# Last pair normalised early, other load orders, and softplus and scan moved into the input projection

## The chip, the cores and the metric

One NeuronCore of a Trainium2 chip runs the whole program. TensorE (PE) multiplies, VectorE (DVE) and ScalarE (ACT) do elementwise work, GpSimd (POOL) and SyncE (SP) mostly issue DMAs. The metric is the device time of one execution in microseconds (us), lower is better.

## What is computed

One inference step of a one-layer hybrid decoder, over 64 sample rows and a prompt of 1024 rows with 16 learned tokens ahead (1152 columns `T` in the kernel, padding among them):

```python
u = rmsnorm(h, norm_mix)
p = u @ w_in                       # conv, shift, gate and dt columns
dt = softplus(dt_raw + dt_bias);  A = -exp(a_log)
acum = cumsum(dt * A)              # within chunks of 128
y_a = rmsnorm((ssd(xs, dt, acum, B, C) + d_skip * xs) * silu(z), ssm_norm)
y_b = (groupnorm(rwkv7(r, decay, k, v, kk, a)) * lnx_w + lnx_b + bonus) * g
h = h + concat(y_a, y_b) @ w_out
h = h + peer(rmsnorm(h))           # product-key experts
y = rmsnorm(h)
```

Outputs are y and the new convolution, shift, SSD and WKV states.

## The kernel before

The program is a row of stages; between two of them all engines meet at a barrier, and SBUF is handed on. Activations lie transposed: 128 channels on the partitions, time in the columns. float32 products are made of three matmuls on rounded halves (`product`, lines 106 to 109: hi*hi, lo*hi, hi*lo); ScalarE makes the rounded high part, DVE the low part.

**Input projection** (`input_projection`, lines 116 to 397). 27 weight tiles of 128 output columns: 8 conv, 14 shift, 4 gate, 1 dt. For each, TensorE makes 72 matmuls of 384 columns (three column blocks `c`, eight row tiles `k`, three each) into one of two PSUM buffers. `over_tiles` hands every engine the same tile order, mostly in loops. SP first loads the norm weights, the eight x tiles and coefficients, then one weight tile at a time. For x tile `k` ScalarE rounds (L243) and squares (L247), DVE makes the low part (L277) and adds pairs of squares (L285), and TensorE sums them over the partitions (L367) into the PSUM buffer of tile 1. In tile 0 the products of block `c=0` follow the x tiles as they come; blocks 1 and 2 come after the last sum. DVE then builds the inverse root mean square (L288, L291), and in `column_work` makes the low part of the next tile's weights (L302) before it scales the finished tile. POOL stores each finished tile to the scratch tensor `cols`.

**SSD** (`ssd_heads`). DVE and ScalarE first form softplus(dt), its decay and a running sum (`tensor_tensor_scan`, L662) on 8 partitions. TensorE waits for that (`dt_step`), spreads the running sums over rows (L790), and turns `dt` and `cum` to rows by 2 x 9 small matmuls (L799, 18 instructions each). Nine chunks of 128 follow.

**RWKV** (`rwkv_heads`). Four head pairs `j`, each with five groups of one or two chunks; a group's triangular inverse takes six merges `l`, and `at_point(l - 0.5)` and `at_point(l)` put other work between them in a fixed order written out per engine. For a pair `j < 3` the group normalisation (mean, centering, square, variance, root, reciprocal, scaling, gating) is placed among the merges of the next pair. The last pair has none behind it, so `tail` does it all at the end: DVE runs `center`, `variance`, `inverse`, `scaled`, `gated` over three column thirds (`thirds`, 384 columns). Semaphores `ep_pe`, `ep_act` and `ep_vec` count these steps, and `reached` turns a step's name to a count.

**Output projection** (`output_projection`, lines 1827 to 1950). SP loads the eight mixed tiles `u` (`y_d`) and then the residual input (`h`, `h_rest`); POOL loads the weight tiles. ScalarE rounds weights 0 and 1, then the eight y tiles. DVE splits weight 0 and the y tiles, waits for `x_loaded` (the residual), and in `add` splits the next weights before it adds a tile to the residual. TensorE does column chunk by column chunk.

The rest (picking experts, spreading gates, experts with 2 x 3 x 2048 matmuls of 352 columns) isn't touched.

Of the kernel before, what the change touches and what calls it, by code (L numbers as in the profile page):

```python
# [26 lines left out]
P = 128  # L27
# [11 lines left out]
IN_TILES = CONV_TILES + SHIFT_TILES + GATE_TILES + 1  # L39
COEFS_IN = 8  # L40
# [75 lines left out]
def input_projection(nc, x_t, norm_g_d, w_pack, coef_d, hist_d, cols_d, new_conv_s, new_conv_p, new_shift_s, new_shift_p):  # L116
    with Stage(nc, "inp") as st:
# [11 lines left out]
        raw = [sb(f"raw_{s}", [P, E_COLS]) for s in range(2)]  # L129
        mid = [sb(f"mid_{s}", [P, T]) for s in range(2)]  # L130
# [19 lines left out]
        edge_stored = [sem(f"edge_stored_{s}") for s in range(2)]  # L150

# [25 lines left out]
        with nc.Block() as block:  # L177
            @block.sync
            def _(sp):
                sp.dma_start(norm_g[:], norm_g_d).then_inc(g_loaded, 16)  # L180
                for k in range(KD):
# [12 lines left out]
            def _(pool):  # L194
# [13 lines left out]
                def store(q, s, m, kind):  # L208
# [17 lines left out]
                    elif kind == "dt":  # L226
                        pool.wait_ge(gate_ready, START + GATE_TILES + 1)
                    else:
                        pool.wait_ge(act_out, START + (m + 1 if kind == "conv" else m + 1 - SHIFT_TILES))
# [9 lines left out]
            def _(act):  # L239
                act.wait_ge(g_loaded, START + 16)  # L240
                for k in range(KD):
                    act.wait_ge(x_loaded[k], START + 16)
                    act.activation(u_hi[:, k, :], u[:, k, :], ACT.Copy, scale=norm_g[:, k:k + 1]).then_inc(u_rounded, 1)  # L243
# [3 lines left out]
                    act.activation(squares[:, k % 4, :], u[:, k, :], ACT.Square).then_inc(square_ready, 1)  # L247
                    if k == 0:
                        act.wait_ge(w_loaded[0], START + 16)
                        act.activation(w_hi[0][:], w[0][:], ACT.Copy).then_inc(w_rounded, 1)  # L250
                act.wait_ge(rms_step, START + 3)
                act.activation(inv_rms[:], inv_rms[:], ACT.Sqrt).then_inc(rms_step, 1)

                def evacuate(q, s, m, kind):
                    if kind != "dt":
# [17 lines left out]
            def _(dve):  # L273
                dve.wait_ge(g_loaded, START + 16)
                for k in range(KD):
# [6 lines left out]
                    if k % 2:  # L282
                        dve.wait_ge(square_ready, START + k + 1)
                        pair = squares[:, k % 4, :]
                        dve.tensor_tensor(pair, squares[:, k % 4 - 1, :], pair, ALU.add).then_inc(pair_ready, 1)  # L285
# [13 lines left out]
                def column_work(q, s, m, kind):  # L299
                    if kind != "dt":  # L300
                        dve.wait_ge(w_rounded, START + m + 2)
                        dve.tensor_tensor(w_lo[1 - s][:], w[1 - s][:], w_hi[1 - s][:], ALU.subtract).then_inc(w_split, 1)  # L302
                    first = isinstance(m, int) and m < 2
                    if kind not in ("conv", "shift"):
# [57 lines left out]
            def _(pe):  # L362
# [7 lines left out]
                def project(q, s, m, kind):  # L370
# [7 lines left out]
                    else:  # L378
# [3 lines left out]
                        else:  # L382
                            pe.wait_ge(raw_ready, START + CONV_TILES + SHIFT_TILES)
                            pe.wait_ge(gate_ready, START + m - (CONV_TILES + SHIFT_TILES) - 1)
                    for c in range(3):
                        for k in range(KD):
                            if first and c == 0:
                                pe.wait_ge(u_split, START + k + 1)
# [2642 lines left out]
```

## Time and profile before

| | us |
|---|---|
| timed runs, median of 3 | 4183.31 (4179.56 to 4183.43) |
| profiled execution, its time | 4152.66 |
| profiled execution, its span | 4151.1 |
| TensorE busy | 3681.1 (89%) |
| DVE busy | 3275.7 (79%) |
| ScalarE busy | 1166.0 (28%) |

The mean granted TensorE clock is 0.936 of full. In the profile a line such as `49.73 0.59 PE L107 ... [3.10 <-DVE ...]` reads: start 49.73 us, duration 0.59 us, engine and source line, then the engine's idle time before it and what ended that. The stages lie at about 0 to 378 us (input projection), 383 to about 545 (SSD), up to 1287 (RWKV), 1292 to 1430 (output projection), then picking, spreading and, from about 2110, experts.

### The profile page before, as it was taken

To read this page: it belongs to the slowest core of one execution; us is meant where nothing else is said; L and a number is where in the kernel's file an instruction comes from. 1 tells how busy PE (TensorE), PEld (TensorE's weight loads), DVE (VectorE), ACT (ScalarE), POOL (GpSimd) and SP (SyncE) were. 2 spreads that over 40 slices of the span, in tenths; PEclk is the share of its full clock that TensorE was granted. 3 is DMA by queue.
4 is the path that set the end of the run, shared out by engine and by line. 5 is a ranking of instruction groups with operands and counts; after the bars stand their busy time and mean duration, and the time that the engine had idled before them with its cause. 6 is when DMAs were issued, how large, how long until landed. Compare 5 with 4: busy or idle time off the path is not lost. (4 is left out here: it accounts for less than half of the span.)

```text
span 4151.1 us, 65513 instructions
## 1 busy us (share of the span) xinstructions
PE 3681.1 (89%) x22408; PEld 3397.2 (82%) x22408; DVE 3275.7 (79%) x6449; ACT 1166.0 (28%) x2129; POOL 1228.1 (30%) x1086
## 2 busy tenths in 40 slices
PE   7997849889895897847769999999999999999997
PEld 6997727777784755537769999999999999999996
DVE  6542746676663389989969999999999999999998
ACT  3102423223221121229932222222222222222221
POOL 1220000000000000000025555555555555555553
PEclk9998758988997999869989999999999999999998
DMA  4573220000003000104478888888888888888885
GB/s 111 89 93 95 76 89 6 23 28 12 1 9 122 22 25 32 52 1 177 196 287 300 297 286 301 294 285 301 290 289 298 295 290 300 292 292 300 288 296 186
DMA packets 291701, 729.32 MB, mean 176 GB/s; under 512 B 27416, under 2 KB 138472, under 8 KB 290048
## 3 DMA queue, kind: packets, MB, share of 16 engines
q0 software_dynamic: 120448, 431.42, 32.4%
q1 hardware_dynamic: 171136, 296.44, 21.1%
q8 instruction: 61, 1.00, 0.1%
q14 instruction: 56, 0.46, 0.0%
HBM read 650.07 MB, written 77.70 MB: 175 GB/s over the span
## 5 line engine op out<-in xcount | busy, mean ns | idle before, releaser
L2565 POOL DMA_INDIRECT experts_u_row<-in_up_rows,experts_u_at x384 | 540.0, 1406 | 642.7 <-DVE experts_dot L2751 527.8
L107 PE MATMUL experts_up_ps<-experts_u_hi,experts_up_hi 128*128 128x352 f32 x2048 | 662.1, 323 | 27.5 <-DVE experts_u_lo L2727 24.8
L107 PE MATMUL experts_down_ps<-experts_act_hi,experts_down_hi 128*128 128x352 f32 x2048 | 676.5, 330 | 8.6 <-DVE experts_down_lo L2727 6.4
L108 PE MATMUL experts_up_ps<-experts_u_lo,experts_up_hi 128*128 128x352 f32 x2048 | 660.9, 323 | 0.0
L109 PE MATMUL experts_up_ps<-experts_u_hi,experts_up_lo 128*128 128x352 f32 x2048 | 660.6, 323 | 0.0
L108 PE MATMUL experts_down_ps<-experts_act_lo,experts_down_hi 128*128 128x352 f32 x2048 | 660.5, 323 | 0.0
L109 PE MATMUL experts_down_ps<-experts_act_hi,experts_down_lo 128*128 128x352 f32 x2048 | 659.8, 322 | 0.0
L2572 POOL DMA_INDIRECT experts_v_row<-in_down,experts_v_at x384 | 513.9, 1338 | 244.8 <-issue 117.6
L2751 DVE CUSTOM_DVE_ANT_0 experts_u_row<-experts_u_row,stream_u_rows_of 128x1024 f32<-128x1024 f32 x384 | 466.3, 1215 | 73.8 <-DMA experts_u_row<-in_up_rows,experts_u_at 72.3
L2764 DVE SCALAR_TENSOR_TENSOR stream_h_rows_of<-experts_v_row,experts_weight,stream_h_rows_of 128x1024 f32<-128x1024 f32 x384 | 497.6, 1296 | 14.4 <-DVE experts_weight L2756 6.8
L2770 DVE TENSOR_TENSOR stream_h<-stream_h,experts_down_ps 128x704 f32<-128x704 f32 x512 | 450.4, 880 | 65.7 <-PE experts_down_ps L109 65.0
L107 PEld LDWEIGHTS experts_down_ps<-experts_act_hi,experts_down_hi 128*128 128x128 f32 x2048 | 385.3, 188 | 35.7 <-DVE stream_h L2770 25.6
L107 PEld LDWEIGHTS experts_up_ps<-experts_u_hi,experts_up_hi 128*128 128x128 f32 x2048 | 385.9, 188 | 30.1 <-issue 22.1
L108 PEld LDWEIGHTS experts_up_ps<-experts_u_lo,experts_up_hi 128*128 128x128 f32 x2048 | 386.4, 189 | 0.0
L109 PEld LDWEIGHTS experts_up_ps<-experts_u_hi,experts_up_lo 128*128 128x128 f32 x2048 | 386.3, 189 | 0.0
L108 PEld LDWEIGHTS experts_down_ps<-experts_act_lo,experts_down_hi 128*128 128x128 f32 x2048 | 386.0, 188 | 0.0
L109 PEld LDWEIGHTS experts_down_ps<-experts_act_hi,experts_down_lo 128*128 128x128 f32 x2048 | 385.7, 188 | 0.0
L2669 ACT ACTIVATE experts_down_hi<-experts_down 128x1024 fp32r<-128x1024 f32 x128 | 135.1, 1055 | 707.9 <-PE experts_down_ps L109 707.9
L2682 ACT ACTIVATE experts_act_v<-experts_up_ps 128x352 f32<-128x352 f32 x256 | 118.8, 465 | 594.2 <-PE experts_up_ps L109 450.3
L2064 PE MATMUL pick_q_ps<-picking_u,pick_w_query 128*128 128x384 f32 (+1 forms) x768 | 252.6, 490 | 25.9 <-DMA pick_sub_keys<-in_keys 17.4
L2064 PEld LDWEIGHTS pick_q_ps<-picking_u,pick_w_query 128*128 128x128 f32 x768 | 150.9, 199 | 118.2 <-issue 41.3
L107 PE MATMUL inp_proj<-inp_u_hi,inp_w_in_hi 128*128 128x384 f32 x648 | 219.5, 339 | 24.9 <-DVE inp_w_in_lo L281 20.2
(396 smaller groups left out, 6497.7 us busy)
## 6 DMA issues: line engine op xcount, KB each, us to landing
experts_up<-in_up SPq DMA_DIRECT2D x128, 512.0 KB
experts_down<-in_down SPq DMA_DIRECT2D x128, 512.0 KB
gates<-spread_spread SPq DMA_DIRECT2D x11, 4096.0 KB, 11.5
experts_gates<-gates SPq DMA_DIRECT2D x64, 704.0 KB
cols<-inp_done POOLq DMA_DIRECT2D x27, 576.0 KB
inp_w_in<-in_w_in SPq DMA_DIRECT2D x27, 512.0 KB
pick_w_query<-in_w_query SPq DMA_DIRECT2D x16, 512.0 KB
experts_u_row<-in_up_rows,experts_u_at POOLq DMA_INDIRECT x384
```

The costliest lines, as they stand in the source:

```text
L107: pe.matmul(out, w_hi, x_hi, start=start, stop=False)
L108: pe.matmul(out, w_hi, x_lo, start=False, stop=False)
L109: return pe.matmul(out, w_lo, x_hi, start=False, stop=stop)
L2064: mm = pe.matmul(q_ps[at_q % 3][:, 0:n], w[s][:, k * P:k * P + P], u[:, k, lo:lo + n], start=(k == 0), stop=(k == KD - 1))
L2565: pool.indirect_dma_start(u_row[b][:], None, up_rows_d, bass.IndirectOffsetOnAxis(ap=u_at[slot][:, b, a:a + 1], axis=0)).then_inc(u_row_lo ...
L2572: pool.indirect_dma_start(v_row[b][:], None, v_table, bass.IndirectOffsetOnAxis(ap=v_at[slot][:, b, a:a + 1], axis=0)).then_inc(v_row_load ...
L2669: act.activation(down_hi[:, e, :], down[e][:], ACT.Copy).then_inc(down_rounded, 1)
L2682: act.activation(act_v[e][:, lo:lo + n], up_ps[e][c][:, 0:n], ACT.Gelu).then_inc(gelu_ready, 1)
L2751: dve.tensor_tensor_reduce(u_row[b][:], u_row[b][:], rows.u[:, b, :], 1.0, 0.0, ALU.mult, ALU.add, dot[slot][:, b, a:a + 1]).then_inc(dott ...
L2764: dve.scalar_tensor_tensor(out=rows.h[:, b, :], in0=v_row[b][:], scalar=weight[slot][:, b, a:a + 1], in1=rows.h[:, b, :], op0=ALU.mult, op ...
L2770: dve.tensor_tensor(row, row, down_ps[m % 2][:, :, 0:DC], ALU.add).then_inc(added, 1)
```

## The change

Four things are changed.

1. *Input projection*: the first weight tile is loaded right after the first x tile; ScalarE squares one x tile behind the rounding; tile 0 is multiplied x tile by x tile for all three column blocks, and the sums of squares lie between those.
2. *dt tile*: it is made before the gate tiles instead of after them; the gate tiles are written out instead of looped. Softplus, decay and scan of dt are done in this stage, on 8 partitions of the x buffer, among the gate tiles. dt and running sum are stored together as 16 rows, and the SSD stage loads them as one tile `dt_cum`; its turning matmuls take both at once (9 instead of 18), and `head_row` has 16 rows.
3. *RWKV, last pair*: mean and variance of the first two thirds go in among the last group's merges; the tail roots, inverts, scales and gates these 768 columns while the last two chunks are computed, and stores them early. The last third follows.
4. *Output projection*: SP loads weight tile 0, then the y tiles, then weight tile 1, then the residual, and also the later weights (POOL did). ScalarE rounds the y tiles before weight tile 1, and tile 0 is multiplied y tile by y tile for all column chunks.

The diff, cut to its core (renamed indices, packing of the weights and the like left out):

```diff
-            for kind, tiles in (("conv", CONV_TILES - 2), ("shift", SHIFT_TILES), ("gate", GATE_TILES)):
+            for kind, tiles in (("conv", CONV_TILES - 2), ("shift", SHIFT_TILES)):
                 with eng.Fori(lo, lo + tiles // 2) as q:
                     for s in range(2):
                         body(q, s, q * 2 + s, kind)
                 lo += tiles // 2
-            body(lo, 0, 2 * lo, "dt")
+            body(lo, 0, DT_TILE, "dt")
+            for m in range(GATE0, IN_TILES):
...
-                for k in range(KD):
+                sp.dma_start(u[:, 0, :], x_t[0]).then_inc(x_loaded[0], 16)
+                sp.dma_start(w[0][:], w_pack[0]).then_inc(w_loaded[0], 16)
+                for k in range(1, KD):
...
+                    if isinstance(m, int) and m == 1:
+                        sp.dma_start(dt_par[:], dt_par_d).then_inc(par_loaded, 16)
+
+                        sp.wait_ge(u_split, START + KD)
+                        sp.wait_ge(sum_done, START + KD // 2)
+                        sp.dma_start(keep, keep_d[0:HEADS, :]).then_inc(par_loaded, 16)
...
+                        pool.wait_ge(dt_step, START + 6)
+                        pool.dma_start(cols_d[m, 0:2 * HEADS, :].rearrange("(a h) t -> h a t", a=2), u[0:HEADS, 0:2, :]).then_inc(stored[s], 16)
+                        return
...
+                    else:
+                        square(k - 1)
+                square(KD - 1)
...
+                    if kind == "dt":
+                        act.wait_ge(par_loaded, START + 32)
+                        act.activation(dt_par[:, 1:2], dt_par[:, 1:2], ACT.Exp).then_inc(dt_act, 1)
+                        act.wait_ge(dt_step, START + 1)
+                        act.activation(dt_abs, dt, ACT.Abs).then_inc(dt_act, 1)
+                        act.wait_ge(dt_act, START + 2)
+                        act.activation(dt_abs, dt_abs, ACT.Exp, scale=-1.0).then_inc(dt_act, 1)
...
+                        if m == GATE0:
+                            act.wait_ge(dt_step, START + 2)
+                            act.activation(dt_abs, dt_abs, ACT.Ln).then_inc(dt_act, 1)
...
+                    if kind == "gate" and m == GATE0:
+                        dve.wait_ge(dt_act, START + 3)
+                        dve.tensor_scalar(dt_abs, dt_abs, 1.0, None, ALU.add).then_inc(dt_step, 1)
+                    if kind == "gate" and m == GATE0 + 1:
+                        dve.wait_ge(dt_act, START + 4)
+                        dve.scalar_tensor_tensor(out=dt, in0=dt, scalar=0.0, in1=dt_abs, op0=ALU.max, op1=ALU.add).then_inc(dt_step, 1)
+                        dve.wait_ge(dt_step, START + 3)
+                        dve.memset(dt[:, NS:P - META], 0.0).then_inc(dt_step, 1)
+                        dve.wait_ge(dt_step, START + 4)
+                        dve.tensor_scalar(log_decay, dt, dt_par[:, 1:2], -1.0, ALU.mult, ALU.mult).then_inc(dt_step, 1)
+                        dve.wait_ge(dt_step, START + 5)
+                        dve.tensor_tensor_scan(cum, keep, log_decay, 0.0, ALU.mult, ALU.add).then_inc(dt_step, 1)
...
+                    if first:
+
+                        for k in range(KD):
+                            pe.wait_ge(u_split, START + k + 1)
+                            for c in range(3):
+                                one(c, k)
+                            if k % 2 == 0 and k:
+                                sum_of_squares(k - 1)
+                        sum_of_squares(KD - 1)
+                        return
...
-                pe.wait_ge(dt_step, 6)
+                pe.wait_ge(dt_loaded, 16)
...
-                        for a, src in enumerate((dt, cum)):
-                            for t in range(NT):
-                                mm = pe.matmul(small_ps[:, a, t, :], src[:, tile_cols(t)], eye[0:HEADS, 0:HEADS], start=True, stop=True)
+                        for t in range(NT):
+                            mm = pe.matmul(by_row_ps[:, t, :, :].rearrange("p a h -> p (a h)"), dt_cum[:, tile_cols(t)], eye[0:2 * HEADS, 0:2 * HEADS],
+                                           start=True, stop=True)
...
+EARLY_PE = {"mean0": 0.5, "var0": 2.5, "mean1": 3.5, "var1": 5}
+EARLY_ACT = {"square0": 1.5, "square1": 4.5}
+EARLY_VEC = {"mean0": 1, "var0": 3, "mean1": 4, "var1": 5.5}
+LAST_MADE = {
+    EP_PE: (*EARLY_PE, "mean2", "var2"),
+    EP_ACT: (*EARLY_ACT, "rooted_early", "square2", "rooted"),
+    EP_VEC: (*EARLY_VEC, "inverse0", "inverse1", "scaled_early", "affine_early", "with_bonus_early", "gated_early",
+             "mean2", "var2", "inverse2", "scaled", "affine", "with_bonus", "gated"),
+}
...
+                    if j == PAIRS - 1:
+                        first_col = 2 * CH
+                        pool.wait_ge(ep_vec, reached(EP_VEC, j, "gated_early"))
+                        pool.dma_start(y_out[:, 0:NS], y_of[x][:, 0:NS]).then_inc(y_stored, 16)
+                        pool.dma_start(y_out[:, NS:NS + first_col - P], y_of[x][:, P:first_col]).then_inc(y_stored, 16)
...
+                    root(last.j, "var1", slice(0, 2 * CH))
                     for a in range(2):
                         copy_rhs(last.ci + a)
                         copy_u(last.ci + a)
                         copy_y(last, a)
-                    for c in range(3):
-                        square(last.j, c)
-                    root(last.j)
+                    square(last.j, 2)
+                    root(last.j, "var2", slice(2 * CH, T))
...
+                    j, early, rest = last.j, slice(0, 2 * CH), slice(2 * CH, T)
+                    inverse(j, 0)
+                    next_state(last, 0)
+                    inverse(j, 1)
+                    scaled(j, early, "inverse1")
+                    next_state(last, 1)
+                    affine(j, early, "_early")
+                    gated(j, early, "_early")
                     center(j, 2)
                     variance(j, 2)
-                    for c in range(3):
-                        inverse(j, c)
-                    scaled(j)
-                    gated(j)
+                    inverse(j, 2)
+                    scaled(j, rest)
+                    affine(j, rest)
...
+                sp.dma_start(w[0][:], w_out_d[0]).then_inc(w_loaded[0], 16)
                 for k in range(KD):
                     sp.dma_start(u[:, k, :], y_d[k]).then_inc(y_loaded[k], 16)
+                sp.dma_start(w[1][:], w_out_d[1]).then_inc(w_loaded[1], 16)
                 sp.dma_start(h[:], x_kept_d[:, :, 0:DENSE].rearrange("k p t -> p k t")).then_inc(x_loaded, 16)
                 sp.dma_start(h_rest[:], x_kept_d[:, :, DENSE:KEPT].rearrange("k p t -> p k t")).then_inc(x_loaded, 16)
+
+                def load(q, s, m):
+                    if isinstance(m, int) and m < 2:
+                        return
+                    sp.wait_ge(w_split, START + m - 1)
+                    sp.dma_start(w[s][:], at(w_out_d, m)).then_inc(w_loaded[s], 16)
+
+                over_tiles(sp, load)
 
...
-                            mm = product(pe, out[s][c][:, 0:n], w_hi[s][:, cut], w_lo[s][:, cut],
-                                         y_hi[:, k, lo:lo + n], y_lo[:, k, lo:lo + n], k == 0, k == KD - 1)
-                        mm.then_inc(out_done, 1)
+                            pe.wait_ge(y_split, START + k + 1)
+                            for c in range(len(OUT_CHUNKS)):
+                                one(c, k)
+                        return
+                    for c in range(len(OUT_CHUNKS)):
+                        for k in range(KD):
+                            one(c, k)
...
-                    if isinstance(m, int) and m == 1:
+                    if isinstance(m, int) and m == 0:
                         for k in range(KD):
                             act.wait_ge(y_loaded[k], START + 16)
                             act.activation(y_hi[:, k, :], u[:, k, :], ACT.Copy).then_inc(y_rounded, 1)
```

## Rows read from the trace of the kernel before

**Rows 1.** The page of the profile, section 1, its busy times

```profile
PE 3681.1 (89%) x22408; PEld 3397.2 (82%) x22408; DVE 3275.7 (79%) x6449; ACT 1166.0 (28%) x2129; POOL 1228.1 (30%) x1086
```

**Rows 2.** Busy time, granted clock and DMA of four stretches, with the header

```profile
core 0: us, PE busy (x) PEld busy (x) DVE busy (x) ACT busy (x) POOL busy (x), PEclk, DMA share, GB/s
10.00:12.00 2.00, 0.00 (x0) 0.00 (x0) 0.00 (x0) 0.00 (x0) 0.00 (x0) 1.00 1.01 408
110.00:170.00 60.00, 60.00 (x348) 60.00 (x348) 37.22 (x58) 8.47 (x8) 14.48 (x21) 1.00 0.52 95
400.00:420.00 20.00, 18.30 (x87) 17.35 (x86) 7.99 (x18) 9.24 (x23) 0.00 (x0) 0.50 0.02 5
1240.00:1245.00 5.00, 5.00 (x47) 4.71 (x47) 2.18 (x6) 1.78 (x6) 0.00 (x0) 1.00 0.01 3
```

**Rows 3.** Timeline of ACT and DVE, 0 to 50 us (start, duration, engine, line)

```profile
5.66 1.28 ACT L243 ACT_TABLE_LOAD   x1 [5.66 <-DMA inp_u<-in_x_t]
17.85 1.06 ACT L250 ACTIVATE inp_w_in_hi<-inp_w_in 128x1024 fp32r<-128x1024 f32 x1 [8.59 <-DMA inp_w_in<-in_w_in]
...
34.40 1.28 ACT L252 ACT_TABLE_LOAD   x1
38.34 1.49 DVE L288 TENSOR_SCALAR inp_inv_rms<-inp_proj 128x384 f32<-128x384 f32 x3 [2.30 <-PE inp_proj L367]
41.06 7.35 DVE L291 RECIPROCAL inp_inv_rms<-inp_inv_rms 128x1152 f32<-128x1152 f32 x1 [1.24 <-ACT inp_inv_rms L252]
48.45 1.23 DVE L302 TENSOR_TENSOR inp_w_in_lo<-inp_w_in,inp_w_in_hi 128x1024 fp32r<-128x1024 f32 x1
```

**Rows 4.** Timeline of PE, 26 to 56 us

```profile
27.47 2.10 PE L367 MATMUL inp_proj<-inp_squares,inp_in_ones 128*128 128x384 f32 x6
...
49.73 0.59 PE L107 MATMUL inp_proj<-inp_u_hi,inp_w_in_hi 128*128 128x384 f32 x1 [3.10 <-DVE inp_w_in_lo L302]
...
53.31 0.34 PE L109 MATMUL inp_proj<-inp_u_hi,inp_w_in_lo 128*128 128x384 f32 x1
```

**Rows 5.** Timeline of ACT at 95 us and of POOL at 378 us

```profile
95.35 1.17 ACT L265 ACTIVATE inp_done<-inp_mid 128x1152 f32<-128x1152 f32 x1 [10.35 <-DVE inp_mid L343]
...
378.07 0.53 POOL L230 DMA_DIRECT2D cols<-inp_done  x1 [10.38 <-DVE inp_done L297]
```

**Rows 6.** Start of the SSD stage: timeline of PE and SP, then DMA issues

```profile
396.96 3.78 PE L790 MATMUL ssd_rows_ps<-ssd_cum,ssd_head_row 8*128 8x128 f32 x16 [19.78 <-DVE ssd_cum L662]
400.53 3.84 PE L799 MATMUL ssd_shared_ps<-ssd_eye,ssd_dt 8*128 8x8 f32 x18
387.40 0.43 SPq L556 DMA_DIRECT2D ssd_ssd_par<-in_ssd_par  x1
ssd_xbc<-cols SPq DMA_DIRECT2D x3, 512.0 KB, 4.8
```

**Rows 7.** End of the RWKV stage: timeline of ACT, DVE and POOL

```profile
1253.33 0.28 ACT L1202 ACTIVATE rwkv_rhs<-rwkv_chain_ps 128x128 f32<-128x128 f32 x1 [1.42 <-PE rwkv_chain_ps L1662]
...
1264.66 0.29 DVE L1438 TENSOR_TENSOR rwkv_s<-rwkv_s_new_part,rwkv_s_kept 128x128 f32<-128x128 f32 x1
1272.68 7.38 DVE L1463 RECIPROCAL rwkv_inv_decay<-rwkv_inv_decay 128x384 f32<-128x384 f32 x3 [1.23 <-ACT rwkv_inv_decay L1228]
...
1281.48 0.88 DVE L1470 TENSOR_SCALAR rwkv_y<-rwkv_y,rwkv_pair_par 128x1152 f32<-128x1152 f32 x1
...
1283.79 1.36 DVE L1477 TENSOR_TENSOR rwkv_y<-rwkv_y,rwkv_gate 128x1152 f32<-128x1152 f32 x1
1286.03 0.54 POOL L1127 DMA_DIRECT2D mixed<-rwkv_y  x1
```

**Rows 8.** Output projection: timeline of SP and DVE

```profile
1292.41 3.86 SPq L1858 DMA_DIRECT2D picking_u<-mixed  x8
...
1321.51 1.23 DVE L1924 TENSOR_TENSOR outp_w_out_lo<-outp_w_out,outp_w_out_hi 128x1024 fp32r<-128x1024 f32 x1 [5.12 <-DMA picking_h_rest<-in_x_kept]
...
1325.20 0.55 DVE L1945 TENSOR_TENSOR picking_h_rest<-picking_h_rest,outp_out 128x384 f32<-128x384 f32 x1 [1.60 <-PE outp_out L109]
```

More of the change, by code:

```diff
@@ L129, in input_projection @@
         raw = [sb(f"raw_{s}", [P, E_COLS]) for s in range(2)]
+        dt_par = sb("dt_par", [HEADS, 2])
+        dt, cum, keep, dt_abs, log_decay = (u[0:HEADS, k, :] for k in range(5))
         mid = [sb(f"mid_{s}", [P, T]) for s in range(2)]
@@ L254, in evacuate @@
                 def evacuate(q, s, m, kind):
-                    if kind != "dt":
+                    if not (isinstance(m, int) and m == IN_TILES - 1):
                         act.wait_ge(w_loaded[1 - s], START + (q + 1 + s) * 16)
@@ L274, in _, with add_pair @@
                 dve.wait_ge(g_loaded, START + 16)
+                def add_pair(k):
+                    dve.wait_ge(square_ready, START + k + 1)
+                    pair = squares[:, k % 4, :]
+                    dve.tensor_tensor(pair, squares[:, k % 4 - 1, :], pair, ALU.add).then_inc(pair_ready, 1)
                 for k in range(KD):
@@ L299, in column_work @@
                 def column_work(q, s, m, kind):
-                    if kind != "dt":
+                    if not (isinstance(m, int) and m == IN_TILES - 1):
                         dve.wait_ge(w_rounded, START + m + 2)
@@ L789, in rows @@
                     for hh in range(HEADS):
-                        mm = pe.matmul(rows_ps[:, hh, :], head_row[:, hh, :], cum[:, tile_cols(c)], start=True, stop=True)
+                        mm = pe.matmul(rows_ps[:, hh, :], head_row[:, hh, :], dt_cum[:, tile_cols(c)], start=True, stop=True)
                     mm.then_inc(rows_done, 1)
@@ L1262, in at_point @@
                         root(group.j - 1)
+                    if after is None:
+                        for c in range(2):
+                            if point == EARLY_ACT[f"square{c}"]:
+                                square(group.j, c)
                 def tail(last):
+                    root(last.j, "var1", slice(0, 2 * CH))
                     for a in range(2):
@@ L1508, in at_point @@
                             scaled(group.j - 1)
+                            affine(group.j - 1)
                         if point == 5:
                             gated(group.j - 1)
-                def tail(last):
-                    for a in range(2):
-                        next_state(last, a)
-                    j = last.j
-                    center(j, 0)
-                    center(j, 1)
-                    variance(j, 0)
-                    variance(j, 1)
+                    if after is None:
+                        for c in range(2):
+                            if point == EARLY_VEC[f"mean{c}"]:
+                                center(group.j, c)
+                            if point == EARLY_VEC[f"var{c}"]:
+                                variance(group.j, c)
+                def tail(last):
+                    j, early, rest = last.j, slice(0, 2 * CH), slice(2 * CH, T)
[6 more added lines that the diff above has]
+                    gated(j, early, "_early")
                     center(j, 2)
                     variance(j, 2)
-                    for c in range(3):
-                        inverse(j, c)
-                    scaled(j)
-                    gated(j)
+                    inverse(j, 2)
+                    scaled(j, rest)
+                    affine(j, rest)
+                    gated(j, rest)
                 over_groups(dve, prepare, start, merge, at_point, tail)
@@ L1768, in at_point @@
                             start_from_samples(after)
+                    else:
+                        for c in range(2):
+                            if point == EARLY_PE[f"mean{c}"]:
+                                mean(group.j, c)
+                            if point == EARLY_PE[f"var{c}"]:
+                                variance(group.j, c)
                     if group.g == 0 and group.j > 0:
@@ L1781, in tail @@
                         make_state(last, a)
-                    j = last.j
-                    mean(j, 0)
-                    mean(j, 1)
-                    variance(j, 0)
-                    variance(j, 1)
-                    mean(j, 2)
-                    variance(j, 2)
+                    mean(last.j, 2)
+                    variance(last.j, 2)
                 over_groups(pe, prepare, start, merge, at_point, tail)
```

183 lines of the change are left out of this document (86 added, 97 removed).

## The prediction

> **What bounds the kernel now.** Read the page first [rows 1]: TensorE is busy 89% of the span, so only what shortens TensorE's path, or the gaps in it, moves the end. The table of stretches [rows 2] says where it is the bound: 110 to 170 us (steady input projection) holds 348 matmuls back to back, 0.172 us each, 12.4 us for the 72 of a weight tile, at the full level (1.00, 2.4 GHz). There an edit on another engine is worth nothing. The change works at four places where TensorE waits for a chain on other engines: the input projection's head [rows 3, 4], the seam to the SSD stage [rows 5, 6], the RWKV stage's end [rows 7], the output projection's head [rows 8]. Experts, picking and the middle of every stage are left as they are, so gains at seams go straight into the time.
>
> **Input projection, head.** Now the first weights land behind all eight x tiles, and ScalarE rounds them at 17.85; the last sum of squares is read at 38.34; 3 column passes (1.49), root, reciprocal (7.35) and the low part of tile 1's weights (1.23) follow, and TensorE starts tile 1 at 49.73 after 3.10 idle [rows 3, 4]. After: x0 lands at 5.66 as now; at 408 GB/s [rows 2] 512 KB take 1.3 us and 576 KB 1.45 us, so w0 is there at 7.0 and the last x at 17. ScalarE: x0 (begun 6.9) 1.2, w0 1.06, DVE's low part 1.23 (behind the 1.4 us x0 pass): TensorE starts at 11. All 72 products of tile 0 (12.4 us) and 24 matmuls of sums (2.10 for six [rows 4], 8.4) now lie before the last sum: 20.8 us. The start is at the half level (1.2 GHz); [rows 4] show one such start: matmuls of 0.59 at 49.73 and of 0.34 at 53.31, thus some 3.6 us at half speed, 1.8 us lost. Sum read at 11 + 20.8 + 1.8 = 33.6. ScalarE isn't later: its remaining passes took 34.40 - 18.9 = 15.5 us, and from 9.2 would end near 26. Gain 38.34 - 33.6, taken as 4.8 (the 2.10 holds some pipeline tail). The chain behind it stays serial, so tile 1 moves by the same 4.8. Its gap grows from 3 to 11.5 us, but 3.1 us already cost the fall to the half level, so I add nothing. Ends: 3 (half level for 7 us) and 6.5.
>
> **The dt tile and softplus, moved.** Tile 22 is now dt, gates are 23 to 26. SP issues one keep load (after the last sum) and dt_par; tile 2's weight load waits behind them to about 36 and is needed only when tile 2's weights are rounded, near 53. ScalarE gets Exp, Abs, Exp, Ln with table loads (1.28 each [rows 3]) and DVE about 6 us: in tiles of 12.4 us, where DVE is busy 37 of 60 us in the conv tiles [rows 2] and less in gate tiles; next tile's weight split comes before this work on DVE, and the first rounding behind it on ScalarE is ready some 6 us into the tile. POOL's dt store waits for the scan, and gate tile 23's store queues behind it; DVE's tile 24 waits for that landing, about 10 of 12.4 us into the tile. Cost nothing; without that cover a few us. But the last tile is now a gate: its Silu (1.17) and hand-off lie between the last product and the last store, which went at 378.07 straight from DVE [rows 5]. Cost 1.2.
>
> **SSD head.** TensorE starts at 396.96, released by the scan, after 19.78 idle [rows 6]. After, it waits for dt_cum and six constants. The last of them was issued at 387.40, with two loads fewer ahead now 386.8; the strided 512 KB load just ahead of it takes 4.8 to land [rows 6] from 385.8, or 390.6. I take 390.8: gain 6.2. Ends: 2 us after issue (+7.6 rather than 6.2), 7 us after (+3). Then 18 matmuls of 8x8 in 3.84 us [rows 6] vanish: the two rows of 18 become one. Gain 3.8; TensorE is at half level there (0.50 [rows 2]) and the next ScalarE copy waits for it, so it is on the path. The level stays low after: the gap is still 14 us.
>
> **RWKV, end.** Now the last state is ready at 1264.95, then mean, square, variance, root, three reciprocals (7.38) and four full-width passes in a row, ending 1283.79 + 1.36 = 1285.15 [rows 7]. After, statistics of two thirds lie in the last group's six merges. There TensorE is full (5.00 of 5 us, 0.95 of it weight loads [rows 2]), so the eight added matmuls cost: at 0.35 each [rows 4] 2.8, less the pauses they fill and pipelining; I take 2.2, ends 0.8 and 4. ScalarE does the early root (two thirds of 1.17 is 0.8, behind a 0.6 variance) before the copy that ran at 1253.33 [rows 7], and the whole chain of the last two chunks queues behind that: 1.1. State ready at 1264.95 + 3.3 = 1268.3. Two reciprocals (2.46 each) and the scaling fit in DVE's waits for TensorE. Then DVE runs the early affine and gating ahead of the last centering (0.6 + 1.8), then per third: center 0.56, square 0.52, variance matmuls 1.0, read 0.56, root 0.52, reciprocal 2.46, four passes 1.8, and 0.6 of hand-offs: 10.4, end 1278.7. Gain 6.4. The store is one POOL issue (0.54) shorter and smaller, about 0.5: 7.5 in all. Ends 4 and 10.
>
> **Output projection, head.** The tempting sum is large: weights first and row by row, tile 0 would end some 10 us sooner. But the second tile's low part is released at 1321.51 by the landing of the residual input (DVE idle 5.12 <- DMA picking_h_rest [rows 8]), since DVE's queue holds that wait ahead of the split. Its landing is set by bytes: y, two weight tiles and 4.25 MB of residual. Only the third weight tile (512 KB, 1.3 us) now comes behind it. So tile 1 starts near 1321.4 instead of the end of tile 0 (1325.0, read by the row at 1325.20): 3.5. Tile 0 ends about 1314.5, TensorE idles 7 us and restarts at the half level, 1.7 by [rows 4]. Gain 1.8. Ends 0.5 and 4. The Trainium skill, "TensorE: Matmul & The Clock Gate", section "HAM oscillation — how this bites in real kernels", warns of the order used here: matmul bursts parted by waits for transfers can run cold each time. By that rule tile 0, whose rows come one transfer at a time, would run at the half level throughout and end near 1324 instead of 1314.5, with no gap behind it: a gain of 1 to 2, much as above. The trace shows one cold restart after one gap and no repeated ones.
>
> **Sum.** 4.8 - 1.2 + 6.2 + 3.8 + 7.5 + 1.8 = 22.9 us. The profiled execution (span 4151.1, time 4152.66) would go to 4129.8. The timed runs have a median of 4183.31, 30.6 us above it, which the profile doesn't explain; I carry the difference over: 4183.3 - 22.9 = **4160.4**.
>
> **Rivals.**
> (a) *The overlaps are thinner*: the last constant lands 7 us after issue (-3.2), the merges take the full 4 us (-1.8) and the output head gives 0.5 (-1.3), the input head 3 (-1.8): gain 14.8, time 4168.5; with the early root holding up the chain by 3 us more, 4171.5. For it: TensorE is full in 1240 to 1245 [rows 2]. Against: all four at once.
> (b) *The output projection keeps its full gain*, because the residual isn't what ends last there: 9 us instead of 1.8, time 4153. For it: TensorE would be ready. Against: the release in [rows 8].
> (c) *Slower by the clock*: the two new long gaps (11.5 and 7 us) are followed by stretches that stay at the half level. From 400 to 420 us TensorE was busy 18.3 of 20 us and still at 0.50 [rows 2]. A dense tile at that level costs 12.4 us more; two tiles behind each gap make 49.6 less the 3.5 counted: 4206. It turns the sign from 46 us at half speed more than counted (23 lost). Against: the dense restart of [rows 4] was back at 53.31.
> (d) *It hardly shows*: the 30.6 us between the profiled and the timed runs move with something outside the edits and swallow it: 4180.
>
> **How the numbers follow.** Forecast 60% (4154 to 4166), (a) 18%, (b) 8%, (d) 10%, (c) 4%. A measurement tells 0.2%, 8.4 us, from no change. Faster: 60 + 18 + 8 = 86%, and 1 of (d): 87%. Same 9%, slower 4%. The range leaves out (c) and most of (d), and takes in (a)'s end and a little beyond (b): 4147 to 4175.
>
> **What the profile after would show.** Sum read near 33.6, tile 1 at 45, with half-level matmuls behind both; DVE's scan inside the gate tiles and no TensorE gap there; SSD's first matmul within some 8 us of that stage's first load, then 18 small matmuls, not 36; the last gating pass about 10 us behind the last state, where it now ends 20 us behind it, and one POOL issue after it; DVE still released by picking_h_rest before tile 1, with TensorE idle 7 us. It would be wrong if a matmul gap opened inside the tiles 22 to 26, if the last constant or the residual landed elsewhere than taken, or if TensorE stayed low after a gap.

## The result

| kernel, job | median (us) | runs from .. to | ratio to before, 95% |
|---|---|---|---|
| before, first job | 4183.37 | 4179.56 .. 4186.96 | |
| after, first job | 4149.69 | 4144.40 .. 4155.00 | 0.992 (0.9905 to 0.9935) |
| before, second job | 4155.67 | 4147.42 .. 4160.22 | |
| after, second job | 4126.44 | 4125.25 .. 4134.40 | 0.9939 (0.9925 to 0.9953) |

The forecast was 4160.4, a gain of 22.9 us, with a range of 4147 to 4175. The first job gives 33.7 us (27 to 40 by the interval), the second 25.3 (20 to 31). The forecast time was 11 us too high; the gain agrees with the second job.

**The profile after** (its own time 4148.04, span 4146.5). First the input projection's head, timeline of PE and DVE (start, duration, engine, line, tiles, idle time before and what ended it):

```profile
31.68 2.10 PE L431 MATMUL inp_proj<-inp_squares,inp_in_ones 128*128 128x384 f32 x6
...
45.20 0.69 PE L109 MATMUL inp_proj<-inp_u_hi,inp_w_in_hi 128*128 128x384 f32 x1 [11.42 <-DVE inp_w_in_lo L344]
33.82 1.49 DVE L330 TENSOR_SCALAR inp_inv_rms<-inp_proj 128x384 f32<-128x384 f32 x3 [4.94 <-PE inp_proj L431]
36.53 7.35 DVE L333 RECIPROCAL inp_inv_rms<-inp_inv_rms 128x1152 f32<-128x1152 f32 x1 [1.23 <-ACT inp_inv_rms L279]
43.92 1.23 DVE L344 TENSOR_TENSOR inp_w_in_lo<-inp_w_in,inp_w_in_hi 128x1024 fp32r<-128x1024 f32 x1
```

The sum is read at 33.82 and tile 1 starts at 45.20; forecast were 33.6 and 45, against 38.34 and 49.73 in [rows 3, 4]. The seam to SSD, PE and SP:

```profile
411.79 3.75 PE L834 MATMUL ssd_rows_ps<-ssd_dt_cum,ssd_head_row 16*128 16x128 f32 x16 [14.60 <-DMA ssd_ssd_par<-in_ssd_par]
415.34 3.86 PE L842 MATMUL ssd_shared_ps<-ssd_eye,ssd_dt_cum 16*128 16x16 f32 x18
419.12 1.11 PE L849 MATMUL ssd_x_ps<-ssd_eye,ssd_xbc 128*128 128x128 f32 x4
404.81 0.33 SPq L605 DMA_DIRECT2D ssd_dt_cum<-cols  x1
```

TensorE is now released by a constant, not by the scan of [rows 6], 6.98 us after the stage's first load, and one row of 18 small matmuls is left. The RWKV end, DVE and POOL, which answers [rows 7]:

```profile
1273.75 0.29 DVE L1503 TENSOR_TENSOR rwkv_s<-rwkv_s_new_part,rwkv_s_kept 128x128 f32<-128x128 f32 x1
...
1280.53 2.55 DVE L1528 RECIPROCAL rwkv_inv_decay<-rwkv_inv_decay 128x384 f32<-128x384 f32 x1 [0.59 <-ACT rwkv_inv_decay L1289]
...
1284.82 0.56 DVE L1545 TENSOR_TENSOR rwkv_y<-rwkv_y,rwkv_gate 128x384 f32<-128x384 f32 x1
1285.67 0.58 POOL L1188 DMA_DIRECT2D mixed<-rwkv_y  x1 [6.61 <-DVE rwkv_y L1545]
```

From the last state (1273.75) to the last gating pass (start 1284.82) it is 11.07 us, where [rows 7] have 19.13, and one issue follows. The output projection's head, SP, PE and DVE, which answers [rows 8]:

```profile
1291.54 0.33 SPq L1936 DMA_DIRECT2D outp_w_out<-in_w_out  x1
1299.69 0.63 PE L109 MATMUL outp_out<-outp_y_hi,outp_w_out_hi 128*128 128x352 f32 x1 [20.35 <-DVE outp_y_lo L2021]
1320.84 0.66 PE L109 MATMUL outp_out<-outp_y_hi,outp_w_out_hi 128*128 128x352 f32 x1 [7.67 <-DVE outp_w_out_lo L2016]
1319.56 1.23 DVE L2016 TENSOR_TENSOR outp_w_out_lo<-outp_w_out,outp_w_out_hi 128x1024 fp32r<-128x1024 f32 x1 [10.38 <-DMA picking_h_rest<-in_x_kept]
```

As forecast, tile 1 waits 7.67 us for the residual input's landing through VectorE's queue. All that stands as the prediction has it. One thing doesn't. Busy time and granted clock by stretch, after:

```profile
core 0: us, PE busy (x) PEld busy (x) DVE busy (x) ACT busy (x) POOL busy (x), PEclk, DMA share, GB/s
150.00:200.00 50.00, 50.00 (x290) 50.00 (x289) 22.31 (x36) 4.25 (x4) 8.84 (x13) 1.00 0.83 82
200.00:250.00 50.00, 46.75 (x267) 45.81 (x266) 19.34 (x33) 3.17 (x3) 11.37 (x16) 1.00 0.81 83
250.00:300.00 50.00, 44.30 (x243) 43.26 (x242) 19.68 (x31) 4.23 (x4) 9.43 (x14) 0.97 0.75 85
300.00:350.00 50.00, 39.29 (x216) 39.00 (x216) 19.18 (x31) 4.84 (x6) 10.47 (x15) 0.90 0.81 77
```

From 200 us on TensorE is no longer full in the shift tiles, which the change leaves alone. Six gaps between 210 and 296 us make 8.95 us, and one of 10.71 stands at the start of tile 22, the dt tile. PE and DVE there:

```profile
332.72 0.66 PE L109 MATMUL inp_proj<-inp_u_hi,inp_w_in_hi 128*128 128x384 f32 x1 [10.71 <-issue]
331.07 0.23 DVE L389 TENSOR_TENSOR inp_raw<-inp_proj,inp_inv_rms 128x64 f32<-128x64 f32 x1 [9.12 <-DMA inp_raw<-in_hist]
```

The SSD stage's first load is at 404.81, where before has 383.49. The input projection thus lost 21 us in this profile although its head gained, and yet the timed runs gained 34. This had to be explained first.

### The profile page after: what moved, and what is told of

The parts are those of the page before. It is cut to its first block and busy times, and to the rows that moved or that the text cites. A ratio compares the mean times of both kernels' runs of the same rounds, so it can differ in the third digit from the quotient of the medians.

```text
span 4146.5 us, 65409 instructions
## 1 busy us (share of the span) xinstructions
PE 3671.6 (89%) x22390; PEld 3391.5 (82%) x22390; DVE 3275.0 (79%) x6453; ACT 1167.4 (28%) x2131; POOL 1226.1 (30%) x1079
## 6 DMA issues: line engine op xcount, KB each, us to landing
gates<-spread_spread SPq DMA_DIRECT2D x11, 4096.0 KB, 11.5
```

## Experiments

**Whose are the gaps, and which part gains what.** e1 is before unchanged, e2 after unchanged, e3 and e4 the two halves of the change. All four ran on one chip.

> The kernel before, once more, for its trace on the chip of the other runs. Theory A (the gaps of TensorE in the shift tiles, some 24 us between 200 and 345 us in the profile after, belong to the chip: its small transfers are slower): they stand in this trace as well, the last product of the input projection ends 20 to 40 us later than in the profile before (377), and the time is near 4180. Theory B (the changed order of loads or the tile moved makes them): no gaps here, the input projection ends near 377 and the time is near 4153.

> The kernel after, once more. Theory A: the gaps in the shift tiles are as in e1, and the ratio to before is 0.994 (23 us, the sum of the prediction). Theory B: the gaps are here alone, the gain is what is left of 23 us after them, a few us.

> Only the changes of the input projection (order of loads, row by row, softplus and scan there) and of the SSD head; the RWKV end and the output projection as before. By the sum of the prediction 4.8 - 1.2 + 6.2 + 3.8 = 13.6 us faster than before. If the moved work slows the tiles (Theory B) it is 5 us faster or slower than before.

> Only the RWKV end and the output projection; the rest as before. By the sum 7.5 + 1.8 = 9.3 us faster. If the two traces read so far are right that the output projection's stage is as long as before, 7.5; if the merges pay their full four us and the projection nothing, 5.

```diff
 # e3: rwkv_heads and output_projection as before, the rest as after
 # e4: rwkv_heads and output_projection as after, the rest as before
```

Measured: e1 4161.08 (one run). e2 0.9939. e3 4138.97, 0.9961 (0.9948 to 0.9975), 16.2 us faster, for 13.6 expected. e4 4148.44, 0.9984 (0.9975 to 0.9993), 6.7 us faster, for 9.3 expected by the sum, or 7.5 or 5; its interval, 3 to 10 us, doesn't choose among them. The halves add up to 22.9, e2 has 25.3. The same stretches in e2:

```profile
150.00:200.00 50.00, 50.00 (x290) 50.00 (x289) 22.93 (x37) 4.25 (x4) 11.04 (x16) 1.00 0.63 91
200.00:250.00 50.00, 50.00 (x291) 50.00 (x290) 22.85 (x37) 4.25 (x4) 11.40 (x16) 1.00 0.71 91
250.00:300.00 50.00, 50.00 (x290) 50.00 (x289) 22.75 (x37) 4.25 (x4) 11.36 (x16) 1.00 0.72 92
300.00:350.00 50.00, 49.30 (x285) 49.01 (x284) 20.73 (x28) 12.10 (x12) 6.83 (x10) 1.00 0.42 70
```

The same code has no gaps here, so the moved tile and the new order of loads don't make them (theory B falls). e1 has none before 300 us either, and its time is 4161 and not 4180, so theory A doesn't hold for this chip. It is the first job that was slower, for both kernels (before by 28 us, after by 23). What differs is a chain in GpSimd's queue. In each conv and shift tile it waits for the previous tile's columns to land, loads the next tile's history (12 byte pieces), stores two edges and then the columns; VectorE can't scale the next tile before that history is there, and its split of the weights after that stands behind the scaling in its queue: it is such a split (L344) that ends the six smaller gaps. Of the 22 history loads that follow the first one, the second and the last, in after and in e2:

```profile
61.59 0.91 POOL L222 DMA_DIRECT2D inp_raw<-in_hist  x1 [7.46 <-DMA cols<-inp_done]
340.85 0.91 POOL L222 DMA_DIRECT2D inp_raw<-in_hist  x1 [9.99 <-DMA cols<-inp_done]
```

```profile
61.20 0.95 POOL L222 DMA_DIRECT2D inp_raw<-in_hist  x1 [7.28 <-DVE inp_raw L339]
313.70 0.91 POOL L222 DMA_DIRECT2D inp_raw<-in_hist  x1 [8.17 <-DMA cols<-inp_done]
```

Over 20 tiles that is 13.96 us a tile in after and 12.62 in e2; in before it is 12.74 and in e1 12.62. A tile's products take 12.48 us. So in each of these profiles the chain is slower than TensorE, and eats up the lead that it starts with. At 12.62 that costs e2 nothing yet: the gap in its last row is 0.70 us at the dt tile, and e9 to e11 below have the same 0.70 there without the chain's wait. At 13.96 the lead is gone by 210, and the stage ends 24.3 us later (404.81 against 380.53).

Why the largest gap stands at the dt tile is in the code. In the shift tiles TensorE waits for the scaling of the tile before the last one (`raw_ready`, `m - 1`), at the dt tile for that of the last shift tile (`CONV_TILES + SHIFT_TILES`), so whatever VectorE lags behind shows there in full: in the two lines above it scales until 332.6, and TensorE starts at 332.72. The kernel before has the same wait at its first gate tile. The dt tile writes the PSUM buffer that tile 20 used, so the looser wait looks sufficient there; no run tried it.

**Does that chain do it?** e7 and e8 lengthen it by one more small load a tile, in after and in before.

```diff
                         pool.dma_start(at(out_p, i), raw[s][:, E_COLS - HIST:E_COLS]).then_inc(edge_stored[s], 16)
+                        load_spare(s, m)      # hist_d[m] once more, into a spare buffer
```

> The kernel after, with one more small transfer (a second load of the 12 byte pieces of the history, into a spare buffer) in each of the 22 conv and shift tiles, so that the chain of small transfers in GpSimd's queue is longer. Theory A (the gaps of the shift tiles in the first profile of after come from this chain, once it is longer than a tile's 12.48 us): gaps of the same kind appear here, of 1 to 3 us a tile in the 14 shift tiles, 15 to 40 us in all. Rival: the chain has more slack, the tiles stay back to back and the time is after's.

> The kernel before with the same extra transfer. Theory A (the chain is no part of the change): it loses as much as e7 does against after, within 5 us. Theory B (the change brought the kernel nearer to this edge): before loses at least 10 us less than after does.

Measured: e7 4134.47, 0.9959 (0.9944 to 0.9974), against 0.9939 without the load: 8 us lost. e8 4158.41, 1.0014 (1.0004 to 1.0024): 6 us lost. In both the period is 13.03 and the SSD stage's first load comes later, at 387.06 for e7 (e2 380.53) and 389.29 for e8 (e1 384.53). Gaps inside the shift tiles, as theory A of e7 has them, don't come: the chain grew by 0.4 us a tile only, and TensorE waits once, at the start of tile 22, for 4.34 us in e7 (0.70 in e2) and 5.29 in e8 (0.84 in before), behind a history load. The loss is smaller than the 15 us expected as the least. It is alike in both kernels within the intervals, so nothing says that the change is nearer to this edge than before was. A period near 14, with gaps in the tiles, wasn't made on purpose by any run.

e10 to e12 take away one wait of that chain. The history's target is free without it, since the queue has by then waited for VectorE and for the edge stores that read it.

```diff
                             pool.wait_ge(edge_stored[1 - s], (q + s) * 32)
-                            pool.wait_ge(stored[1 - s], (q + s) * 16)
```

> The kernel after without that wait alone. Theory: on a chip where after has no gaps in its shift tiles nothing is to be had but the 0.7 us at the dt tile: after's time, 0.994 of before. On a chip as that of the first profile it gives back the 24 us of gaps. Rival: more small transfers in flight at a time slow each other, and the time is up to 5 us above after's.

> The kernel before without that wait. Theory: the profile before has 0.8 us and its second run 2 us of TensorE gaps ahead of the last shift tile, so 1 to 3 us faster than before; on a chip as that of the first timed runs of before, 25 to 30 us. Rival: no difference.

> e7 (one more small transfer a tile) without that wait. Theory (the wait on the columns is the link that ends last in the chain): the 8 us that e7 lost come back, the period of the history loads falls from 13.03 to 12.5 us, the gap at the end of the shift tiles goes. Rival (the small transfers set the pace): the period stays near 13.0, the time is e7's, 0.996 of before.

Measured: e10 4132.0, 0.9952 (0.9938 to 0.9966). e12 4153.5, 1.0003 (0.9994 to 1.0012). e11 4134.99, 0.9961 (0.9948 to 0.9973). None is faster than its partner by time, and e10 lies 5 us above e2, where its rival has it. The traces say more. GpSimd's waits from 60 to 320 us (total, times, longest), first e2, then e9 below, which has the wait away too:

```profile
POOL inp_raw L222 <- DMA cols<-inp_done: 165.0, 19, 12.1
POOL cols L250 <- ACT inp_done L292: 19.0, 6, 4.0
```

```profile
POOL inp_raw L222 <- DVE inp_raw L346: 123.1, 14, 9.1
POOL inp_raw L222 <- DMA out_conv_p<-inp_raw: 46.2, 6, 10.0
```

Without the wait the chain follows VectorE: the period is 12.49 in e10 and e12, and 12.63 in e11, where e7 had 13.03. e11's SSD stage starts 4.8 us sooner than e7's (382.22 against 387.06). That it isn't faster by time comes with stretches outside the edit: from the first x product of SSD to the last RWKV group it took 817.5 us, e7 810.4, and from the output projection's tile 2 to the end 6 us more than e7. e7's gap of 4.34 at the dt tile is back to 0.70. So the wait is the link that ends last. By itself its removal is worth nothing where the chain runs at 12.6: from tile 1's start to the last product e10 takes 328.2 us and e2 327.9, and both have the 0.70 at the dt tile, which e10's theory wanted to win. e10's profiled execution is 4.0 us longer than e2's, and the stretch from SSD's first x product to the last RWKV group, outside the edit, is 5.1 longer (815.9 against 810.8), so its time doesn't speak for the rival either. e12 shows no difference, as its rival says. What the removal is worth where the chain runs at 14 wasn't tried, since no later job ran so.

**What the head is worth.** e6 rounds and splits weight tiles 1 and 2 ahead of the root and the reciprocal.

```diff
                 square(KD - 1)
+                act.wait_ge(w_loaded[1], START + 16)
+                act.activation(w_hi[1][:], w[1][:], ACT.Copy).then_inc(w_rounded, 1)
                 act.wait_ge(rms_step, START + 3)
...
                 add_pair(KD - 1)
+                split_in(1, 1)                # VectorE: low part of tile 1
                 dve.wait_ge(sum_done, START + KD // 2)
```

> The kernel after, with the second and third weight tiles of the input projection rounded and split ahead of the root and the 7.35 us reciprocal (ScalarE runs one weight tile further ahead from there on). TensorE then starts tile 1 when the sums have been read, near 35.2 in place of 45.0, without the 11.4 us gap, and at the full level. Theory (the reciprocal ahead of the split in VectorE's queue is what the head is worth, and the clock costs 2.2): tile 3 starts 10 to 12 us earlier and the time is 10 to 12 us below after's. Rival (the moved tail is a chain on VectorE anyway, since it must scale tiles 0 and 1 before their banks are free): the gap comes back at tile 2 or 3, 4 us or less.

Measured: 4129.47, 0.9942 (0.9929 to 0.9955), no faster than e2. Timeline of PE in e6, the start of tile 1 and the gap at the dt tile, then DVE at that gap:

```profile
35.77 0.41 PE L109 MATMUL inp_proj<-inp_u_hi,inp_w_in_hi 128*128 128x384 f32 x1 [1.67 <-DVE inp_inv_rms L338]
306.94 0.66 PE L109 MATMUL inp_proj<-inp_u_hi,inp_w_in_hi 128*128 128x384 f32 x1 [6.50 <-issue]
305.29 0.22 DVE L398 TENSOR_TENSOR inp_raw<-inp_proj,inp_inv_rms 128x64 f32<-128x64 f32 x1 [8.30 <-DMA inp_raw<-in_hist]
```

The 11.4 us gap of the head is gone and tile 1 starts 9.2 us sooner. But the SSD stage's first load is at 378.72, only 1.8 sooner than in e2. The lead is given back at 306.94, where VectorE had waited 8.30 us for a history load. Two small gaps near 112 and 138 us take 1.5 us more. Neither theory named this place. The chain's first load hangs on the inverse root (47.25 in e6, near 46.7 in e2), which e6 left where it was, so TensorE ran ahead of a chain that didn't start earlier, and the strict wait at the dt tile collected the whole lag.

**The output projection's gap.** e5 splits the second weight tile before the wait for the residual; e9 is e5, e6 and the wait taken away.

```diff
                     dve.tensor_tensor(y_lo[:, k, :], u[:, k, :], y_hi[:, k, :], ALU.subtract).then_inc(y_split, 1)
+                split_w(1, 1)
                 dve.wait_ge(x_loaded, START + 32)
```

> The kernel after, with one line moved: VectorE splits the second weight tile of the output projection before it waits for the residual input. In the second run of after TensorE idles 8.68 us between tile 0 and tile 1 there, released by that split, and restarts at the half level, which costs 2.4 us more. Theory (the wait in VectorE's queue holds tile 1): the idle time and the restart vanish, 9 to 11 us faster than after, 34 to 36 us faster than before. Rival (the transfer itself, or the adds that free the result banks, hold the third tile at the same time as now): the gap moves behind tile 1, and the time is after's, within 2 us.

> e5 and e6 together, and GpSimd no longer waits for the landing of the previous tile's columns before it loads the next tile's history. Theory (the gap that e6 showed before the last shift tiles is the small-transfer chain in GpSimd's queue, 12.65 us a tile against 12.48 of TensorE, and that wait is what ends last in it): the input projection keeps the 12 us of e6's head, its last product falls near 362, no gap before the dt tile, and the time is 45 to 49 us below before. Rival (the small transfers themselves set the pace, wait or no wait): the gap stays as in e6, and the time is 36 to 39 us below before, as e5 and e6 add up to.

Measured: e5 4114.66, 0.9915 (0.9897 to 0.9933), 35.3 us faster than before. Timeline of PE in e2 and in e5, every wait over 1 us behind the first product of the stage:

```profile
1274.97 0.63 PE L109 MATMUL outp_out<-outp_y_hi,outp_w_out_hi 128*128 128x352 f32 x1 [19.66 <-DVE outp_y_lo L2021]
1297.43 0.66 PE L109 MATMUL outp_out<-outp_y_hi,outp_w_out_hi 128*128 128x352 f32 x1 [8.68 <-DVE outp_w_out_lo L2016]
1315.54 0.43 PE L109 MATMUL outp_out<-outp_y_hi,outp_w_out_hi 128*128 128x352 f32 x1 [3.73 <-DVE picking_h_rest L2037]
```

```profile
1273.71 0.63 PE L109 MATMUL outp_out<-outp_y_hi,outp_w_out_hi 128*128 128x352 f32 x1 [20.09 <-DVE outp_y_lo L2021]
1302.77 0.43 PE L109 MATMUL outp_out<-outp_y_hi,outp_w_out_hi 128*128 128x352 f32 x1 [3.73 <-DVE picking_h_rest L2038]
```

From the first product to tile 2's it was 40.57 us and is 29.06, 11.5 less: the 8.68 us gap, 2.4 us of half level behind it (tile 1's first product to tile 2's takes 18.11 and 15.76 us) and 0.5 in tile 0. The rival (the gap moves) falls.

e9: 4110.92, 0.9903 (0.9889 to 0.9918), 40 us faster than before, the fastest of all. Its time lies between the two expectations and doesn't decide; the trace does. Its SSD stage's first load is at 368.62, 11.9 us sooner than e2's and 10.1 sooner than e6's: the wait that is worth nothing by itself is worth 10 us once TensorE has a lead to keep. TensorE's stretches are full but for the 0.70 us at the dt tile, where e6 has 43.50 of 50 in the last:

```profile
200.00:300.00 100.00, 99.30 (x573) 99.01 (x572) 45.51 (x74) 8.49 (x8) 22.92 (x33) 1.00 0.71 91
300.00:350.00 50.00, 50.00 (x290) 50.00 (x290) 18.55 (x23) 13.76 (x13) 3.61 (x6) 1.00 0.30 59
```

## Why the prediction was right, step by step

The table takes each term between two events that exist in both kernels. Before is taken from up to five profiles (before, e1, e3, e4, e8 and e12, each where that stretch is as before), after from up to eight; the first line goes without the kernels whose small transfers were edited, and without the first job's. The last column is the difference of medians.

| stretch (us) | before | after | forecast | measured |
|---|---|---|---|---|
| start to SSD's first load | 383.5 to 384.5 | 380.5 to 381.6 | 3.6 | 3.8 |
| that load to the first SSD product | 13.5 to 13.6 | 6.9 to 7.8 | 6.2 | 6.4 |
| from there to the first x product | 11.18 | 7.33 | 3.8 | 3.85 |
| first level join of the last RWKV group to the projection's first load | 64.6 to 68.5 | 60.8 to 61.4 | 7.5 | 5.7 |
| that load to tile 2's first product | 48.3 to 50.8 | 47.4 to 48.0 | 1.8 | 1.6 |
| sum | | | 22.9 | 21 |

So every stretch moved the way that was forecast. The sum in the traces is 21 us, the timed gains are 25.3 and 33.7.

- **Input head**: tile 1 starts 4.53 us sooner, for 4.8 taken, and the last Silu with its hand-off costs 1.3 (6.3 and 7.6 us from the last product to SSD's first load), for 1.2. The half level behind the longer gap was mis-sized a little: some 14 matmuls come 0.32 us apart from 45.20 to 49.85, about 2.2 us lost for the 1.8 taken. It was right that a gap of 3 us already costs the fall to the half level, but the longer gap wasn't quite free.
- **The moved softplus and scan** cost nothing, as forecast. VectorE's tile 24 waited for the landing of the scan's store until 348.00 in e2, and TensorE had no gap there.
- **SSD head**: 6.4 for 6.2 and 3.85 for 3.8. One end of the range is off by its own numbers: a constant that lands 2 us after its issue at 386.8 gives 8.2 us, and not 7.6. Nothing rests on it.
- **RWKV end**: against the one profile that the forecast had, two costs were mis-sized and cancel, which is luck. The eight matmuls in the merges cost 2.67 us, first to last join of the group, 24.06 before and 26.73 after in every profile (2.2 taken). The early root cost 0.15 (16.65 to 16.80 from there to the last state, 1.1 taken). State to end of gating fell by 8.9 (9.8 taken), the store by 1.1 (1.1). Against [rows 7] that is 7.1. The spread of before, which the forecast didn't know, makes it 5.7 at the median. The stretch from the last join to the last state goes with the granted clock: with the old RWKV code 16.65 us at 0.70 in before and e1, 14.4 to 14.5 at 0.87 in e8 and e12, 13.2 at 1.00 in e3; with the new code 16.7 to 17.3 at 0.72 to 0.74 in all nine profiles. So the new order may have cost up to 2.4 us there (median 14.5 against 16.9) by keeping the tail from its better executions; that it does isn't shown by five profiles against nine. The rows are before's 1250:1260 and e3's 1239:1249:

```profile
1250.00:1260.00 10.00, 8.01 (x48) 6.60 (x47) 2.27 (x8) 1.88 (x6) 0.00 (x0) 0.74 0.00 0
```

```profile
1239.00:1249.00 10.00, 7.61 (x62) 6.19 (x61) 2.28 (x8) 2.16 (x7) 0.00 (x0) 1.00 0.00 0
```

- **Output head**: the release was named rightly, and its size holds only at the median. In after tile 1 starts 29.3 us after the first load and tile 0 of before ended at 32.8, 3.5 as forecast, but the restart costs 2.6 for 1.7 (18.4 us from tile 1's first product to tile 2's, 15.8 in before). Against before's own profile only 0.7 is left. Against e1 it is 2.6, because there tile 0 ran at 0.50 to 0.53 up to 1325; in after's order it is at 1.00 from 1305. The Trainium skill, "TensorE: Matmul & The Clock Gate", section on HAM oscillation, warns that bursts parted by waits for transfers run cold each time. By that rule tile 0 of after, whose rows come one transfer at a time, would have stayed at the half level. The trace doesn't show that, and doesn't test the rule either: TensorE was busy without such waits, and the clock was up 3 us after the tile's start (first row after's, second e1's, where tile 0 began at 1313.9):

```profile
1305.00:1310.00 5.00, 5.00 (x32) 5.00 (x31) 3.99 (x4) 3.44 (x4) 0.00 (x0) 1.00 1.02 402
```

```profile
1320.00:1325.00 5.00, 5.00 (x16) 4.18 (x17) 2.17 (x2) 0.00 (x0) 0.00 (x0) 0.53 1.05 376
```

- **The 30.6 us carried over** from the profiled to the timed runs was right to carry, though the prediction knew no reason for them and didn't name the chain: that it slowed both kernels alike was in part luck. The likeliest reason is the chain: with 1.2 to 1.3 us more a tile over some 20 tiles it makes 24 to 27 us. It was seen at 13.96 in after's profile of that job; before has no trace from that job, so for before it is an inference. The transfers themselves were slower in that profile: the 12 KB edge store of the shift tiles took 8.4 us at the median from issue to landing, for 7.2 in e2 and e1 and 7.7 in before. Whether the chip or something else slows them isn't shown.
- **What stays open**: the first job's gain is 33.7, 11 us above the forecast, of which its interval leaves 4 at least. No edit explains it. A stretch that the change doesn't touch, from SSD's first x product to the last RWKV group, took 808 to 828 us over the fourteen profiles. Its median is 815.8 in the five with the old input head and 811.1 in the nine with the new one; with spreads of 8 and 19 us these runs don't tell whether that favours one kernel. Steps of this size sit on every single comparison here, and e1 against e2 holds one of 9 us.
- **Rivals**: (b) would have needed e5's edit, since the residual did end last. (a), (c) and (d) didn't come: no stretch stayed at the half level behind the two new gaps, and the changes showed in each stretch.

## What to carry to other kernels

Follow a head's gain to the end of its stage before you count it: where a second chain, here 22 rounds of small transfers at 12.6 us against 12.48 of TensorE, has almost the same period, a lead won by TensorE alone is given back at the stage's end (e6), while one won ahead of both is kept. Look where it is given back: a wait that is one step stricter than its neighbours, as at the dt tile, collects all the lag. A wait that stands in an in-order queue ahead of unrelated work is the first thing to look for behind a gap: moving one split ahead of one wait (e5) gave 10 us, more than the whole RWKV edit (5.7). And when the profiled run lies 30 us off the timed ones, carry the difference over but look for a stretch with hardly any slack, since a slower run shows there.

## What was not expected of the hardware

- The period of the same small-transfer chain in the same kernel was 12.62 us in one job and 13.96 in another. The kernel's time moved by 23 us with it.
- With TensorE's work unchanged, its tail in RWKV took 13.2, 14.4 to 14.5 or 16.65 us from the last join to the last state, at a granted clock of 1.00, 0.87 or 0.70; which one depended on the execution.
- In the column order of the kernel before, the output projection's tile 0 stayed at 0.50 to 0.53 for 11 us in e1, though TensorE counts as busy throughout; in the row order of after it was at 1.00 after 3 us.
- One more load of 12 KB in 12 byte pieces per tile raised the period by only 0.4 us, though GpSimd's issue of it alone takes 0.91.
